# Cache copies issued by GpSimd in pieces of two rows instead of three, in a two-layer decoder trunk

## The reference

```python
DEPTH, D_MODEL, SEQ, DEC_BATCH, PAST_LEN = 2, 1024, 256, 8, 2048
C_CONV, C_POOL, C_ATT, HEAD_DIM = 384, 256, 384, 64

def trunk_layer(x, start_pos, conv_buf, pool_buf, k_buf, v_buf, ...):
    h = rms_norm(x, norm_g)
    proj = jnp.einsum('btd,de->bte', h, w_in)          # 1024 -> 3200 columns
    a_val, a_glu, a_gate, b_val, b_gate, q, k, v, c_gate = split(proj)
    # A: GLU -> causal depthwise conv (31) -> LayerNorm -> swish, gated
    # B: trailing means over 2/4/8/16 positions, per-group map, gated
    # C: dilated attention over offsets 0..128, 0..512 step 4, 0..2048 step 16, gated
    kk = jnp.concatenate([k_buf, k], axis=1)
    vv = jnp.concatenate([v_buf, v], axis=1)
    o = dilated_attention(q, kk, vv, k_buf.shape[1])
    new_k, new_v = kk[:, -n_keep:], vv[:, -n_keep:]    # the cache, moved on by one row
    y = jnp.einsum('bte,ed->btd', jnp.concatenate([ya, yb, yc], axis=-1), w_out)
    return x + y, new_conv, new_pool, new_k, new_v
```

## Time and profile before

| | before |
|---|---|
| time, median of 3 runs | 409.22 us (408.93 to 413.0) |
| the profiled execution's own time | 406.74 us |
| its span in the profile | 404.9 us |
| PE / DVE / ACT / POOL busy | 336.8 / 232.5 / 99.3 / 54.2 us |
| moved by the DMA engines | 158.10 MB in 51269 packets, mean 390 GB/s |

### The profile page before, as it was taken

The page is one execution under the profiler, slowest core; times in us unless marked ns, Lnnn a source line. Parts: engine busy times, 40 slices in busy tenths (PEclk is TensorE's granted clock), DMA queues, the critical chain, the costliest instruction groups (busy, mean ns, idle before and its releaser), DMA issues.

```text
span 404.9 us, 4681 instructions
## 1 busy us (share of the span) xinstructions
PE 336.8 (83%) x1546; PEld 267.5 (66%) x1546; DVE 232.5 (57%) x524; ACT 99.3 (25%) x234; POOL 54.2 (13%) x104
## 2 busy tenths in 40 slices
PE   1799999920557897898997999999778996989991
PEld 1588888810435675667886888888556765758881
DVE  1625798401998578753103358988988587662101
ACT  2300215410023333251102001353214332340011
POOL 2710101111111111111011110111111011200000
PEclk9999999975595999999999999999867999999997
DMA  7999999999999999999999999999999999999995
GB/s 289 417 419 419 419 418 416 416 415 379 363 396 394 395 404 414 411 367 393 415 418 417 412 417 418 415 414 386 416 416 383 387 375 399 359 399 359 345 330 196
DMA packets 51269, 158.10 MB, mean 390 GB/s; under 512 B 6356, under 2 KB 18078, under 8 KB 51246
## 3 DMA queue, kind: packets, MB, share of 16 engines
q0 software_dynamic: 21056, 89.61, 56.7%
q1 hardware_dynamic: 20804, 38.60, 25.8%
q10 hardware_dynamic: 9386, 29.60, 18.3%
HBM read 143.91 MB, written 104.42 MB: 613 GB/s over the span
## 4 chain that ended last, share of the span: by engine, by line
PE 49%; DVE 19%; SPq 18%; DMA 6%; ACT 3%; issue 3%; ACTq 0%; DVEq 0%
PE pj L596 21%; PE pj L739 14%; SPq L395 14%; DMA kg<-in_cache_k_win 6%; DVE yc L1157 4%; SPq L435 4%; PE psc L668 4%; DVE tok L1098 3%; DVE ssc L1101 3%; PE ptr L521 3%; DVE spsum_pad L1127 1%; PE ps L716 1%; PE ps L555 1%; ACT sc L903 1%; DVE sc L1065 1%
## 5 line engine op out<-in xcount | busy, mean ns | idle before, releaser
L596 PE MATMUL pj<-hT,wt 128*128 128x264 f32 x800 | 194.1, 401 | 3.0 <-DVE hT L1017 3.0
L596 PEld LDWEIGHTS pj<-hT,wt 128*128 128x128 f32 x800 | 156.6, 199 | 34.7 <-issue 7.3
L1157 DVE SCALAR_TENSOR_TENSOR yc<-u_ext,par,yc 128x256 f32<-128x256 f32 x180 | 76.2, 480 | 2.8 <-DVE u_smp L1045 0.6
L739 PE MATMUL pj<-mix,wt 128*128 128x264 f32 x256 | 59.4, 387 | 0.0
L739 PEld LDWEIGHTS pj<-mix,wt 128*128 128x128 f32 x256 | 48.0, 190 | 7.9
L511 POOL DMA_DIRECT2D out<-in_cache_v_win x48 | 25.8, 544 | 166.0 <-issue 166.0
L511 POOL DMA_DIRECT2D out<-in_cache_k_win x48 | 26.0, 549 | 119.4 <-issue 111.8
L1227 DVE TENSOR_TENSOR xT<-xT,pj 128x264 f32<-128x264 f32 x16 | 6.9, 430 | 53.5 <-PE pj L739 53.5
L1098 DVE TENSOR_TENSOR tok<-kg,qb 128x1536 f32<-128x1536 f32 x10 | 17.6, 1758 | 23.4 <-DMA kg<-in_cache_k_win 22.9
L608 PE MATMUL prt<-sqg,cst 128*128 128x264 f32 x24 | 7.9, 415 | 22.2 <-DVE scr L1028 22.2
L844 ACT ACTIVATE ex<-pj 128x264 f32<-128x264 f32 x22 | 8.6, 391 | 69.6 <-PE pj L596 56.0
(11 more groups left out here) (175 smaller groups left out, 329.3 us busy)
## 6 DMA issues: line engine op xcount, KB each, us to landing
wt<-in_w_tiles ACTq DMA_DIRECT2D x52, 512.0 KB, 8.1
out<-in_cache_k_win POOLq DMA_DIRECT2D x16, 1152.0 KB, 66.2
out<-in_cache_v_win POOLq DMA_DIRECT2D x16, 1152.0 KB, 61.4
out<-in_cache_k_win POOLq DMA_DIRECT2D x17, 1080.0 KB, 70.7
out<-in_cache_v_win POOLq DMA_DIRECT2D x17, 1080.0 KB, 64.7
wt<-in_w_tiles SPq DMA_DIRECT2D x14, 512.0 KB, 21.6
out<-in_cache_k_win POOLq DMA_DIRECT2D x16, 432.0 KB, 72.5
out<-in_cache_v_win POOLq DMA_DIRECT2D x16, 432.0 KB, 66.7
```

What stands on the lines that cost most here:

```text
L596: last = nc.tensor.matmul(pj[n % RING][:, 0:T], wt[:, g % WRING, k, :], hT[:, k, :], start=(k == 0), stop=(k == KD - 1))
L739: last = nc.tensor.matmul(pj[n % RING][:, 0:T], wt[:, g % WRING, k, :], mix[:, k, :], start=(k == 0), stop=(k == KD - 1))
L1157: last = V.scalar_tensor_tensor(out=yc[:, t, 0:SEQ], in0=x_w, scalar=par[:, ROW_CW + w * CT + t:ROW_CW + w * CT + t + 1], in1=yc[:, t, 0:S ...
```

## The change

The copies that GpSimd issues are cut into smaller pieces: two rows (3072 B) instead of three (4608 B) in the contiguous ranges and in the leftovers, and half of a block's three rows (2304 B) in the range of blocks. By the constants' formulas `EVEN_ROWS` becomes 1504 and `ODD_PIECES` 30, and the last leftover is one row instead of two.

```diff
-PIECE_ROWS = 3
+PIECE_ROWS = 2
 FAR_LO, FAR_STEP = GATHER[1][0], GATHER[1][1]
 EVEN_ROWS = (FAR_LO - 1) // (16 * PIECE_ROWS) * 16 * PIECE_ROWS
 ODD_PIECES = (FAR_LO - 1 - EVEN_ROWS) // PIECE_ROWS * PIECE_ROWS
 COPIES = [(kind, s, a, b) for kind in ("k", "v") for s in range(NS)
           for a, b in ((0, 768), (768, EVEN_ROWS), (FAR_LO, GATHER[0][0]))]
 NEAR_BYTES = 2 * C_ATT * 4
+COPY_BYTES = PIECE_ROWS * C_ATT * 4
+BLOCK_BYTES = (FAR_STEP - 1) * C_ATT * 4 // 2
...
-                        dst = out[l, s, a:b].rearrange("(c e f) h d -> c e (f h d)", c=16, f=FAR_STEP)[:, :, 0:PIECE_ROWS * C_ATT]
+                        dst = out[l, s, a:b].rearrange("(c e f) h d -> c e (f h d)", c=16, f=FAR_STEP)[:, :, 0:(FAR_STEP - 1) * C_ATT]
                         src = cache[l, s, a:b].rearrange("(c e f) h d -> c e (f h d)", c=16, f=FAR_STEP)[:, :, C_ATT:FAR_STEP * C_ATT]
-                    pool.dma_start(dst, src, max_dma_last_dim=PIECE_ROWS * C_ATT * 4).then_inc(copy_out[n % IN_FLIGHT], 16)
+                    pool.dma_start(dst, src, max_dma_last_dim=COPY_BYTES if a < FAR_LO else BLOCK_BYTES).then_inc(copy_out[n % IN_FLIGHT], 16)
...
                     pool.dma_start(out[:, a * C_ATT:b * C_ATT], cache[:, (a + 1) * C_ATT:(b + 1) * C_ATT],
-                                   max_dma_last_dim=PIECE_ROWS * C_ATT * 4).then_inc(bulk_out, 16)
+                                   max_dma_last_dim=COPY_BYTES).then_inc(bulk_out, 16)
```

## The result

The changed kernel takes 439.0 us (median of 4 runs, 433.37 to 441.97) against 410.93 us before (408.93 to 413.0, runs of both sets together); the ratio is 1.064 (1.059 to 1.070). The profiled execution took 436.74 us, its span is 434.9 us. The prediction had the sign, slower, but 415.7 us and a range up to 424: 6.5 us of loss were forecast, 28 measured.

A forecast was written before the change was run, and what follows sets the result against it. The prediction took the always busy DMA engines as the bound, with copies ending last. Extra packets 5 us plus slow copies at the end 1.5 gave 6.5 on 409.22, so 415.7 us; own range 412 to 419, overall 406 to 424.

The forecast's parts named there:

- Number of packets: GpSimd's copies on q0: 21056 packets become 32320, 704 more per engine, costing 3.7 to 6.2 us, taken as 5.
- a wait for kg near 20 us: DVE's wait for the layer 0 keys: about 7 us if right; near 20 would mean turns aren't one packet each.
- The turns: Sharing of the DMA engines: q0 and q1 alternate packet by packet whatever the size, 4034 against 4028 from 15 to 100 us.
- The price of a packet: DMA engine time: 36.77 us per MB plus 8.8 ns per packet, 5.3 ns at the lower end.
- The working for the keys: Gather of layer 0 keys: 54.5 ns less per q1 turn, 252 turns per engine, 13.7 to 18 us earlier, taken as 16.
- All later DMA waits were already covered: Compute chain after the keys: no later transfer wait would show, and q1 and q10 would only get more engine time.
- slow stretches of the copies: Copies running alone after compute move 356 GB/s, 10% below busy stretches: 1.5 us lost, between 0 and 4.
- the compute chain and the stores of y end some 16 us earlier: End of the compute chain: the gain at the keys carries through, ending near 388 instead of 404 us.
- GpSimd's issue: GpSimd's 96 copy issues: 54 us become at worst 86, covered by its full ring; landing near 45 us after issue.
- A: Extra q0 packets cost less than their price, half hidden: 1.9 us, no loss at the end, 411.1 us; chance 0.20.
- B: Kernel gets faster: smaller copy turns even out HBM load, recovering 10 of 12 us stretching, 404.2 us; chance 0.12.
- C: Small copies alone at the end lose another 10% against 356 GB/s: 13 us slower, 422.2 us; chance 0.08.

The follow-up runs named there:

- Two edits: Against the kernel before, 3072 B pieces (6144 B packets) in the contiguous ranges of only the first 48 copies, or only the last 48: ratio 1.023 and 1.008.

## Why the prediction was wrong

**The step that failed** is the one on the size of the packets: "Number of packets ... After: (384 + 368 + 192) x 32 = 30208, + 480 + 32 + 1600 = 32320", and with it "The mean packet of q0 shrinks from 4256 B ... to 2773 B". It took a piece of the code for a packet of the engine; the runs showed 17248 packets with a mean of 5195 B. Before the change the two are the same in number, because one piece of 4608 B fills a packet by itself; my count of 21056 matched the row and seemed to confirm it. No row of the trace before could show filling, since its copies had no piece below 4096 B but the 32 of the leftovers, of which each engine has one in a DMA. The Trainium skill, "DMA: Bandwidth & Descriptors", section "SWDGE vs HWDGE vs iDMA", gives for GpSimd's path a packet of preferably up to 4096 B and up to 64 descriptors. The prediction didn't ask what that makes of a piece of 3072 B. The runs show that the packet isn't kept below 4096 B but closed once it has reached it (6144 B from two pieces of 3072, 4608 B from three of 1536, 4096 B from eight of 512). The sign that the prediction named, "a wait for kg near 20 us (then the turns are not one packet each)", was misread in advance too. The turns are one packet each, the packet was another.

**What held.** The price of a packet: the 6144 B packets take 36.77 x 6.144 + 8.8 = 234.7 ns by the prediction's two numbers, and the trace has 234 ns as the median of their durations (251 in the mean; for 4608 B it is 178 and 188). The turns: 3378 against 3377. The working for the keys holds as well when it is given the right packet: 5195 - 4256 = 939 B x 36.77 us per MB = 34.5 ns more per turn, x 252 turns = 8.7 us, up to 11.6 with q10's share; measured 10.8 us. The same formula with the wrong packet gave 16 us earlier instead of 11 later.

**The mechanism of the loss** was the opposite of the one forecast. The forecast's chain ended with copies that had given time away. In fact the copies took the time of SP's transfers: they are through before 400 us, and the compute chain ends with the DMA engines almost idle. "All later DMA waits were already covered, and q1 and q10 only get more" failed with the packet size: the values of layer 1 were covered by 15.6 us, and q1 got less. From 400 to 434 us no packet of q0 is left:

```profile
DMA packets 880, 1.49 MB, mean 44 GB/s; under 512 B 118, under 2 KB 350, under 8 KB 878
...
q1 hardware_dynamic: 878, 1.46, 12.5%
```

The 6.5 us that were forecast and the 28 that came have nothing in common but the sign; that the sign came out right was luck.

**The forecast for a really smaller turn** can be judged by the packets of 4096 B and by SP's whole near rows: compute chain a little earlier, copies last, slower by 0.8% and 2.1%. The direction was right, though not the size: 5 and 7 us on each engine are more packet time of q0, where the forecast had 1.5 us (0 to 4) for slow stretches of the copies. That "the compute chain and the stores of y end some 16 us earlier" was too high a hope in any case: 3.3 us at the keys were 1 us at the stores of y.

**GpSimd's issue** was costed right in kind. It takes 619 ns for the copies of the keys instead of 556, and 46.3 us to landing where 45 were forecast, with 12 copies issued at once; no wait of the compute engines is for it.

**The rivals.** None of A, B or C was the case. What was missing is the rival that "the change doesn't do what it says": that finer pieces may leave the packets as they are, or enlarge them. It should have had a price of its own. Its condition stood in no row, but the price of a packet of two pieces could have been worked out from rows of before: 8.7 to 11.6 us more at the keys alone.

## What to carry to other kernels

While the queues take turns, a queue's weight against the others is the bytes of its packet, not of the piece that the code names. For copies that GpSimd issues, count q0's packets in the profile after each change of size: the piece sizes 1536, 2304 and 4608 B gave the same packet here, 3072 and 6144 B one a third larger, and 4096 B the smallest. In this kernel, whose DMA engines are always busy, the split between queues is what is tuned, and both sides lose: larger turns of the copies starve SP's list (6.4%), smaller ones come with copies that end last (0.8%). An engine that issues long transfers one after the other collects every small delay; compare the landing with the first use to see the room behind it, which was 15.6 us here. A start 13 or 22 us late made no wait for the values, one 45 us late made 20.9 us of it.

## What the runs showed of the hardware that was not expected

- GpSimd's queue fills packets until they hold at least 4096 B, across gaps between rows and within one DMA; what is left at the end of a DMA goes as a smaller packet (512 of 3072 B in the run with pieces of 512 B, 21568 packets in all). SP's queue makes one packet of each piece (4096 more pieces, 4096 more packets).
- Three pieces in a packet of 4608 B in place of one cost 1.9% of the time; the median packet stays at 178 ns, the mean goes from 188 to 195. That the pieces are the cause isn't shown, since the run with SP's larger pieces has 194 ns with one piece a packet.
- SP's pieces of 12288 B go as one packet each too, 1024 of them with a median of 460 ns.
- Two edits that cost 2.3% and 0.8% alone cost 6.4% together, since only together they use up the room of 15.6 us before the values are needed.
